# The tokens of all passes but the last are finished during the last expert pass

## The reference

```python
def moe_swiglu(x, wr, br, w1, w3, w2):
    logits = (x @ wr).astype(jnp.float32) + br.astype(jnp.float32)
    top_val, top_idx = lax.top_k(logits, TOP_K)          # TOP_K = 2
    gates = jax.nn.softmax(top_val, axis=-1)
    combine = jnp.einsum('btk,btke->bte', gates, jax.nn.one_hot(top_idx, N_EXPERTS, dtype=jnp.float32))
    y = jnp.zeros_like(x)
    for e in range(N_EXPERTS):
        h = jax.nn.silu(x @ w1[e]) * (x @ w3[e])
        y = y + (combine[..., e:e + 1].astype(x.dtype) * h) @ w2[e]
    return y
# then, for prompt and sample tokens: x = layer_norm(ALPHA * x + moe_swiglu(x), ln2_g, ln2_b)
```

## Time and profile before

| | before |
|---|---|
| median of 3 runs | 889.21 us (886.07 to 892.51) |
| the profiled execution | 892.3 us |
| its span, first to last instruction | 890.7 us |
| PE busy | 823.4 us (92% of the span) |
| DVE busy | 252.6 us (28%) |
| ACT busy | 137.0 us (15%) |
| POOL busy | 97.2 us (11%) |
| mean granted PE clock | 0.955 |

### The profile page before, as it was taken

The page is one execution under the profiler, slowest core; times in us unless marked ns, Lnnn a source line. Parts: engine busy times, 40 slices in busy tenths (PEclk is TensorE's granted clock), DMA queues, the critical chain, the costliest instruction groups (busy, mean ns, idle before and its releaser), DMA issues.

```text
span 890.7 us, 13881 instructions
## 1 busy us (share of the span) xinstructions
PE 823.4 (92%) x5909; PEld 565.4 (63%) x5909; DVE 252.6 (28%) x700; ACT 137.0 (15%) x336; POOL 97.2 (11%) x142
## 2 busy tenths in 40 slices
PE   6999999999999999999979899999997999999930
PEld 5888878888888888877666567773433354344320
DVE  2173224000000000254585821363111021112108
ACT  0010113000000111132136641120000010000000
POOL 4300300000000000031203400020111001110030
PEclk9999999999999999999988979969998999999975
DMA  9799623637320348992205625937999999999931
GB/s 299 275 375 364 221 83 94 189 115 234 117 79 1 100 148 251 169 261 54 95 28 183 262 124 211 391 157 280 380 410 395 409 393 395 409 395 397 366 106 72
DMA packets 106552, 206.82 MB, mean 232 GB/s; under 512 B 23470, under 2 KB 60698, under 8 KB 105476
## 3 DMA queue, kind: packets, MB, share of 16 engines
q1 hardware_dynamic: 93492, 166.68, 53.1%
q0 software_dynamic: 9376, 32.80, 10.6%
q10 hardware_dynamic: 3632, 6.59, 2.1%
HBM read 192.97 MB, written 13.08 MB: 231 GB/s over the span
## 4 chain that ended last, share of the span: by engine, by line
PE 85%; DVE 7%; DMA 4%; issue 2%; ACT 1%; SPq 1%; POOL 0%; POOLq 0%; DVEq 0%; ACTq 0%
PE ps L652 44%; PE ps L1225 16%; PE ps L1214 8%; DMA slot<-moe_w 2%; PE ps L703 2%; PE ps L1182 1%; PE ps L1039 1%; PE ps L982 1%; PE ps L1055 1%; PE ps L990 1%; PE ps L1008 1%; PE ps L1207 1%; PE ps L865 1%; DVE fin L1867 1%; DMA scr<-r_rows,rowk 1%
## 5 line engine op out<-in xcount | busy, mean ns | idle before, releaser
L1225 PE MATMUL ps<-slot,hT 128*32 128x512 f32 x1408 | 157.3, 606 | 6.0 <-DMA slot<-moe_w 4.7
L652 PE MATMUL ps<-rw,slot 128*128 128x264 f32 x640 | 142.6, 385 | 0.0
L652 PEld LDWEIGHTS ps<-rw,slot 128*128 128x128 f32 x640 | 120.8, 189 | 21.7
L652 PE MATMUL ps<-xw,slot 128*128 128x264 f32 x512 | 120.3, 391 | 0.8 <-issue 0.8
L1225 PEld LDWEIGHTS ps<-slot,hT 128*32 128x32 f32 x1408 | 46.2, 112 | 112.3 <-issue 108.2
L652 PEld LDWEIGHTS ps<-xw,slot 128*128 128x128 f32 x512 | 96.8, 192 | 19.4 <-issue 2.3
L1214 PE MATMUL ps<-slot,hT 128*32 128x256 f32 x1408 | 79.1, 380 | 0.7 <-DMA slot<-moe_w 0.7
L652 PE MATMUL ps<-hT,slot 128*128 128x264 f32 x352 | 79.8, 386 | 0.0
L652 PEld LDWEIGHTS ps<-hT,slot 128*128 128x128 f32 x352 | 66.3, 190 | 10.9
L1214 PEld LDWEIGHTS ps<-slot,hT 128*32 128x32 f32 x1408 | 44.2, 110 | 30.8 <-DMA slot<-moe_w 1.2
L652 PE MATMUL ps<-yT,slot 128*128 128x264 f32 x256 | 59.4, 388 | 0.5 <-ACT yT L1428 0.5
(11 more groups left out here) (416 smaller groups left out, 804.2 us busy)
## 6 DMA issues: line engine op xcount, KB each, us to landing
slot<-moe_w SPq DMA_DIRECT2D x64, 1024.0 KB, 18.5
slot<-moe_w SPq DMA_DIRECT2D x16, 2048.0 KB, 22.5
slot<-ffn_w SPq DMA_DIRECT2D x22, 1024.0 KB, 8.5
slot<-ffn_w SPq DMA_DIRECT2D x8, 1408.0 KB, 6.6
slot<-w_in_even SPq DMA_DIRECT2D x4, 2048.0 KB, 13.6
r_rows<-silu ACTq DMA_DIRECT2D x1, 6144.0 KB, 32.0
slot<-w_out_even SPq DMA_DIRECT2D x2, 2048.0 KB, 23.2
slot<-w_in_odd SPq DMA_DIRECT2D x2, 2048.0 KB, 12.3
```

The lines of the kernel that those rows point to most:

```text
L652: mm = pe.matmul(out, lhs(k), rhs(k), start=(k == 0), stop=(k == n - 1))
L1225: mm = pe.matmul(ps[t][32 * j:32 * j + 32, :].rearrange("p (w n) -> p w n", w=2), xgT[:, cap * k + 32 * t:cap * k + 32 * t + 32], moe_slab ...
```

## The change

All passes but the last are now in the loop (or written out), and the last pass is written out after it. Of what stood after the loop, two things are made.

**Tokens of the other passes.** POOL waits only for the rows of the passes before the last, then issues the six gathers. DVE combines with gates that are zero for rows of the last pass (`ggate`), by `own(t)`, into `xrow`; `stats(t)` and `scale(t)` normalise and SP stores all tiles, also of tokens whose result is not complete. These rows are overwritten later.

**Slots of the last pass.** Behind pass 1 DVE builds selection matrices `lsel` (slot by token) and gates for them. In the last pass PE multiplies `lsel` by a small table (the output row numbers and the gate of each slot's token) and by `xrow` (the combined rows of each slot's token), in strip layout (`own_rows`); ACT copies that to `lown`. As each tile's down projection ends, DVE adds it times the gate (`slot_part`) and takes the statistics of its 256 channels; PE averages them over the four strips (`fold`); DVE normalises (`slot_scale`), with gain and bias in strip layout (`lgb`, loaded early by POOL). POOL then scatters each tile to y_prompt and y_sample in pieces of 256 channels; pieces that belong to the other output or to an empty slot are out of bounds and are dropped. The last pass has no rows of a next pass to transpose or to fetch, its results don't go to `r_rows`.

The core of the diff:

```diff
@@ POOL
+            pool.dma_start(spare[:, 0:P + 10], c_comb[:, NE:NE + P + 10]).then_inc(gb_in, 16)
+            for a, v in enumerate((ln2_g, ln2_b)):
+                for j in range(4):
+                    pool.dma_start(lgb[32 * j:32 * j + 32, a, :],
+                                   v[1:2, 256 * j:256 * j + 256].to_broadcast([32, 256])).then_inc(gb_in, 16)
...
-            with pool.Fori(5, n) as i:
+            with pool.Fori(5, many + 5) as i:
                 one_pass(i, 3)
-            pool.wait_ge(rows_stored, 96 + 64 * n)
+            pool.wait_ge(rows_stored, 96 + 64 * (many + 5))
...
+            pool.wait_ge(y_stored, 48)
+            for u in range(3):
+                pool.wait_ge(final_ready, u + 4)
+                for which, rows in enumerate((TP, TS)):
+                    pool.indirect_dma_start(out=cells[which], out_offset=bass.IndirectOffsetOnAxis(
+                                                ap=cell[:, u, which:which + 1].bitcast(U32), axis=0),
+                                            in_=orow[:, u, :], in_offset=None, bounds_check=4 * rows - 1,
+                                            oob_is_err=False).then_inc(slot_stored, 16)
@@ PE, in one_pass
+                if not after:
+                    own_rows()
                 arrived(5)
                 for t in range(nt):
                     for m in range(4, KD):
                         mm = down(t, m)
                     mm.then_inc(w2_done, 1)
+                    if not after and t:
+                        fold(t - 1)
+            def own_rows():
+                pe.wait_ge(gb_in, 208)
+                pe.wait_ge(lsel_ready, 3)
+                for u in range(3):
+                    for t in range(3):
+                        m = P if t < 2 else 8
+                        mm = pe.matmul(ps[2][:, 4 * u:4 * u + 3],
+                                       lsel[0:m, t, u].rearrange("p j s -> p (j s)"),
+                                       tab[0:m, t, :], start=(t == 0), stop=(t == 2))
+                pe.wait_ge(own_ready, 3)
+                for u in range(3):
+                    for t in range(3):
+                        m = P if t < 2 else 8
+                        for j in range(4):
+                            mm = pe.matmul(ps[u // 2][32 * j:32 * j + 32, 256 * (u % 2):256 * (u % 2) + 256],
+                                           lsel[0:m, t, u, j], xrow[0:m, t, 256 * j:256 * j + 256],
+                                           start=(t == 0), stop=(t == 2))
+                    if u:
+                        mm.then_inc(lown_done, 1)
+            def fold(u):
+                pe.wait_ge(lpart, u + 1)
+                pe.matmul(ps[(3, 7, 2)[u]][:, 16:18], fold4, lfin[:, u, 6:8], start=True, stop=True).then_inc(lfold, 1)
...
+            one_pass(many + 5, 3, None)
+            fold(2)
@@ DVE
+            def own(t):
...
+                dve.wait_ge(res_in[t], 32)
+                then(V.scalar_tensor_tensor(out=a, in0=a, scalar=ggate[0:m, 0, t:t + 1], in1=xrow[0:m, t, :],
+                                            op0=ALU.mult, op1=ALU.add))
+                V.scalar_tensor_tensor(out=xrow[0:m, t, :], in0=b, scalar=ggate[0:m, 1, t:t + 1], in1=a,
+                                       op0=ALU.mult, op1=ALU.add).then_inc(own_ready, 1)
...
             for t in range(3):
-                centre(t)
+                own(t)
+            stats(0)
+            base = tiles_at(many + 5)
+            for t in range(3):
+                dve.wait_ge(gated, base + t + 1)
+                V.tensor_tensor(hmid[:, t, :], silug[:, t % 2, :], ps[t][:, 256:512], ALU.mult).then_inc(h_done, 1)
+            stats(1)
+            stats(2)
+            for t in range(3):
                 scale(t)
...
+            slot_part(0)
+            slot_part(1)
+            slot_scale(0)
+            slot_part(2)
+            slot_scale(1)
+            slot_scale(2)
```

More of the change, by code:

```diff
@@ L26 @@
 ROUNDS = -(-(TP + TS) // CAP)
+NOCELL = 2048.0
 MAXP = NE + 2 * (TP + TS) // CAP
@@ L464, in _ @@
                 next_expert(i)
-            with sp.Fori(5, n) as i:
+            with sp.Fori(5, many + 6) as i:
                 next_expert(i)
@@ L1237, in one_pass @@
                 hidden_t(1)
-                pe.wait_ge(xg_in, 16 * (i + 1))
-                rows_t(after)
+                if after:
+                    pe.wait_ge(xg_in, 16 * (i + 1))
+                    rows_t(after)
                 arrived(4)
@@ L1257, in _ @@
             one_pass(4, 2, CAP)
-            with pe.Fori(5, n) as i:
+            with pe.Fori(5, many + 5) as i:
                 for s in range(NSLOT):
@@ L1513, in _ @@
             one_pass(4, 2)
-            with act.Fori(5, n) as i:
+            with act.Fori(5, many + 5) as i:
                 one_pass(i, 3)
+            one_pass(many + 5, 3)
             for t in range(3):
@@ L1519, in _ @@
                 act.activation(fin[0:m, t, 14:15], fin[0:m, t, 13:14], ACT.Sqrt, bias=eps[0:m, 0:1]).then_inc(fstd, 1)
+            for a in range(2):
+                act.wait_ge(lown_done, a + 1)
+                act.copy(lown[:, 2 * a:(2, 3)[a], :].rearrange("p u n -> p (u n)"),
+                         ps[a][:, 0:(512, 256)[a]]).then_inc(lown_copied, 1)
+            for u in range(3):
+                act.wait_ge(fvar, u + 4)
+                act.activation(lfin[:, u, 10:11], lfin[:, u, 9:10], ACT.Sqrt, scale=-1.0, bias=eps[:, 0:1]).then_inc(fstd, 1)
         @block.vector
@@ L2136, in _ @@
             for t in range(3):
-                centre(t)
-                scale(t)
+                own(t)
[6 more added lines that the diff above has]
+            stats(2)
+            for t in range(3):
+                scale(t)
+            dve.wait_ge(lown_done, 1)
@@ new lines, in slot_scale @@
+            def slot_scale(u):
+                r = orow[:, u, :]
+                dve.wait_ge(lfold, u + 1)
+                then(V.tensor_copy(lfin[:, u, 12:14], ps[(3, 7, 2)[u]][:, 16:18]))
+                V.scalar_tensor_tensor(out=lfin[:, u, 9:10], in0=lfin[:, u, 12:13], scalar=lfin[:, u, 12:13],
+                                       in1=lfin[:, u, 13:14], op0=ALU.mult, op1=ALU.subtract).then_inc(fvar, 1)
+                then(V.scalar_tensor_tensor(out=r, in0=r, scalar=lfin[:, u, 12:13], in1=lgb[:, 0, :],
+                                            op0=ALU.subtract, op1=ALU.mult))
+                dve.wait_ge(fstd, u + 4)
+                then(V.reciprocal(lfin[:, u, 11:12], lfin[:, u, 10:11]))
+                V.scalar_tensor_tensor(out=r, in0=r, scalar=lfin[:, u, 11:12], in1=lgb[:, 1, :],
+                                       op0=ALU.mult, op1=ALU.add).then_inc(final_ready, 1)
@@ L2184, in constants @@
         query[:, None] % 4 == np.arange(32)[None, :] % 4)
+    comb = np.zeros((P, NE + P + 10), np.float32)
+    comb[:, 0:NE] = row[:, None] % 32 == np.arange(NE)[None, :]
+    comb[:, NE:NE + P] = 0.25 * (row[:, None] % 32 == row[None, :] % 32)
+    comb[:, NE + P] = NOCELL + row // 32 + 0.25
+    for t in range(2):
+        comb[:, NE + P + 1 + 3 * t] = 4 * (P * t + row) - NOCELL
+    comb[0:TS, NE + P + 8] = 4 * row[0:TS] - NOCELL
     digit = np.stack([(row % 16).astype(np.uint32) << np.uint32(28 - 4 * s) for s in range(8)], 1).view(np.int32)
```

79 lines of the change are left out of this document (59 added, 20 removed).

## The result

| | before | after |
|---|---|---|
| median | 888.81 us (4 runs, 886.07 to 892.51) | 900.92 us (4 runs, 898.52 to 902.51) |
| the profiled execution | 892.3 us | 901.13 us |
| its span | 890.7 us | 899.5 us |
| PE busy | 823.4 us | 838.5 us |
| DVE busy | 252.6 us | 259.1 us |

The changed kernel is slower: ratio 1.0125, 95% interval 1.0102 to 1.0149. The forecast was 885 us with a range of 877 to 893. The medians differ by 12.1 us, the profiled spans by 8.8 only, since the profiled execution of the kernel before is close to its slowest. (One execution of the kernel before, of the ten taken beside the eighth experiment, took 2978 us and is left out of the numbers there.)

What follows compares the result with a forecast made beforehand. PE held 85% of the chain that ended last, with 35.6 us behind it. A gain of 18.9 us less 14.6 of stall put the span at 886.4, 4.3 earlier than 890.7: 885 us on the median, range 877 to 893.

Steps and rivals of the forecast that it cites:

- step 7: Tail behind down: slots finished on DVE, six POOL scatters at 1.26 us each, last landing 2.2 us later; end X + 30.3.
- step 5: PE's clock falls to about half in the stall and stays low briefly after work resumes: + 1.9 us, PE ends X + 20.5.
- The gathers' start: On POOL in the last pass, gathers wait only for pass 6's rows: first starts at 831.4, six end at 838.6.
- Their transfer: Gathers beside the weights move at 0.155 MB/us: first pair lands at 842.5, second at 849.2; late weights cost nothing.
- The rule that I quoted: Each DMA engine goes round-robin between queue rows by packet, so gathers and weights share equally: halves of 0.205 MB/us each.
- X: When DVE's first gated product of the last pass can start: 856.1 instead of 841.53.
- DVE in front of the products: own(0..2) and stats(0) wait for gathers ahead of the gated products, delaying the first from 841.53 to 856.1; PE stands idle.
- PE from X on: Down matmuls start at X + 1.35 and take 11.1 us, own_rows between their halves 6.1; PE ends at X + 18.6.
- The slower rival: PE's clock stays at 0.5 to the end of the down matmuls: span 901.5, 900 on the median; chance 7%.
- DVE behind the products: Products, stats, scale and small operations last to X + 13.5, all under PE's 20.5; without that cover up to 12 us.
- early work: Nine small POOL loads and some 3 us of DVE work behind pass 1, in DVE idle time: zero; without cover 3 us.

Runs made afterwards that it cites:

- eighth experiment: The seventh experiment's kernel with POOL starting the six gathers only once PE has begun the down projection: 881.81 us, ratio 0.9909 to the kernel before.
- fifth experiment: The changed kernel with the gated products ahead of own and stats(0) on DVE in the last pass: 893.38 us, ratio 1.0029 to the kernel before.
- sixth: The changed kernel with gated products ahead of own and stats(0), and narrow matmuls ahead of the last pass's up projection: 889.72 us, ratio 1.0015 to before.
- seventh experiment: The changed kernel with late own, and last-pass slots returned to token order on PE instead of scattered by POOL: 883.82 us, ratio 0.9935 to before.
- third experiment: The changed kernel with the nine narrow matmuls of own_rows moved into PE's stall, ahead of the hidden transposes: 892.53 us, span 890.9, one execution.
- first experiment: The changed kernel without POOL's six scatters and SP's wait for them: span 884.0 us, 885.63 in all, one execution.
- fourth experiment: The changed kernel with 21 unused 128 x 256 matmuls on PE ahead of the hidden transposes: 901.3 us, span 898.5, one execution.

## Why the prediction was wrong

The kernel ended at 899.5 us of span where the sum said 886.4. Two steps failed: step 7 left out POOL's end of the program (8.2 us), and step 5 had one low stretch of the clock where there were two (6.5 us). By the steps of the prediction, measured against said:

1. *The gathers' start*: said 831.4, measured 827.66. The stores of pass 6 were issued by 820.97 (818.58 + 2.39) where I took 825.8; most of that is spread between executions, since the fifth experiment's kernel, the same up to there, issued them from 823.16, and the twelve profiles have them between 816.92 and 823.58. The delay behind them was 6.7 us, said 5.6.
2. *Their transfer*: the times behind the start were right, the rate was not. The first `own` started 11.7 us behind the first gather's start (said 11.3), the second 17.8 (said 18.0). This kernel's DMA queues in 832 to 841 us (packets, MB, share):

```profile
q1 hardware_dynamic: 475, 1.89, 52.4%
q0 software_dynamic: 480, 1.77, 49.5%
```

   The gathers had 0.197 MB/us beside the weights' 0.210, not 0.155. The rule that I quoted (the Trainium skill, DMA: Bandwidth & Descriptors, "Queues, rings and completion order") gave that share, and this trace agrees with it: 480 packets beside 475. The landing that I worked out from it, 14.5 us behind the first gather, was about 3 us too early. By 839 q0 had moved 1.40 MB, and only then had the first pair's 1.05 MB landed, which fits gathers that move side by side. The other half of the row is that the weights lose what the gathers get. The step put the late weights at nothing, since X was later anyhow, and in the changed kernel that holds: PE waited 1.50 us for slot 3 at 836.02, ahead of the longer wait for DVE. It costs as soon as X is mended: slot 4 kept PE waiting for 4.24, 3.49 and 4.38 us (fifth, sixth and seventh experiments).
3. *DVE in front of the products*: right in kind and place. X was 851.9, said 856.1, and 3.7 of these 4.2 us are the gathers' start. PE's stall of 10.97 us was released by DVE and was the largest of the pass, said 12 to 14.
4. *PE from X on*: said 18.6 us without the clock, measured 20.5 (28.6 less 8.1). `own_rows` took 7.34 at full clock (2.61 + 4.73), said 6.1. The narrow matmuls were priced by the router's 18 records (2.00), the wide ones by down's 55 ns per record, and they took 66. The first down matmul came 1.72 us behind X (said 1.35). The end of PE's down matmuls before the change is 855.02 (846.18 + 8.84), not 855.06, which changes nothing.
5. *Clock*: said 1.9 us, measured 8.1. The first block lost 1.6 of it, near the 1.9. The other 6.5 came from a second low stretch that no step had: the clock rose at about 857 and fell again between 863 and 864, while `own_rows` ran. PE ended at X + 28.6, said X + 20.5. The slower rival had a clock low to the end of down; what happened is a recovery and a second fall, so its 901.5 is near the measured end by chance. The third experiment ties the second fall to the narrow matmuls, by one execution, and the sixth shows that they don't do it alone.
6. *DVE behind the products* and 8. *early work*: right. DVE finished the last of `scale` at about 866.2, 14.3 us behind X (said 13.5), under PE's work; the block behind pass 1 ended at 658.3, and the next product there came at 668.50 after 10.21 us of idle time.
7. *The slots*: the scatters were right, the end was not. The first issue came 1.8 us behind PE's end (said 1.3), the six took 6.54 us from first to last start (said 6.3), and they were landed at 891.1, 2.3 us after the last one started (said 2.2). Then 8.2 us follow that the sum had left out: POOL's end of the program.

The sum: -4.2 (X), +8.1 (PE), +0.5, +0.2 and +0.1 (slots), +8.2 (POOL's end), and 0.2 to the span's end, together +13.1 on 886.4.

The step that failed worst is 7, the last in time. It took POOL's last DMA to be the end of its work, since it looked only at busy time, at the chain and at what the stores of SP do. The trace of before had the answer: a DRAIN of POOL that ended 9.7 us behind its last gather, which cost nothing only for being under DVE's work. "What covers this, and what if the cover is gone" was asked of each edit, but not of the engine's end. That X came 4.2 us early was luck and hid part of the error. With that one term (8.2) the sum would have been 894.6 of span, slower than before by 0.4%, and with the second low stretch (6.5) 901.1.

## What to carry to other kernels

Look at what each engine does at the end of its program, in the view by source line and for the queues' own instructions, before you give it the last work: on POOL that end took 9.2 us or more here, and a kernel that ends with a POOL DMA, or only with a late wait on POOL, pays most of it. When a transfer is moved ahead to overlap, price what it takes from the transfers beside it, and consider starting it as late as its user allows (the eighth experiment: the weights came in time again, but PE then lost some 4 us while the gathers ran). When a stall on PE is worked out, look for the low clock behind it and for light work soon after the clock's return.

## What the runs showed of the hardware

- POOL's last DRAIN took 9.6 to 9.7 us with nothing outstanding, whether a DMA or only a wait stood before it; 9.2 to 9.7 us counted from the last issue where that was later. Where the six gathers had been issued beside the weights it ended later still: 16.4 us behind their last issue in the first experiment (832.98 to 849.4), 16.1 in the seventh (830.9 + 20.9, last issue ended 835.7); where they were issued later, 9.2 (eighth). Why is open; it is hidden in all three.
- Eighteen records of 128 x 3 matmuls (2.61 us) 3 to 4 us after the clock had risen again were followed by a second low clock, in the changed kernel and in the fourth and fifth experiments; behind a long full stretch they were not (sixth). Which part of the record decides it was not tried.
- A gap of 1.7 us on PE behind 9.3 us of filling, with short work behind the gap, was followed by a fall of the clock about a microsecond after work resumed (fourth experiment).
- While six gathers filled the DMA engines to 88%, PE took 11.3 us for 128 records that took 7.11 without them, at a granted clock of 1.00 in both (eighth and seventh experiments). The cause is open.
- Behind the last issue of a pass's stores POOL stood 2.5 us until they had landed with idle queues (861.15 less 858.63) and 6.3 to 6.7 us beside the weights.
